# Eight of twelve modulation blocks formed by GpSimd in the weight ring instead of by TensorE

## The reference, cut to what matters

```python
mod = jax.nn.silu(c) @ w_ada[l] + b_ada[l]            # c: (1, 1024), w_ada: (1024, 6144)
shift1, scale1, gate1, shift2, scale2, gate2 = jnp.split(mod, N_MOD, axis=-1)
h = modulate(rms_norm(x, norm1_g[l]), shift1, scale1)
proj = h @ w_in[l]                                     # 5120 columns: q, k, v of two attentions, two gates
...                                                    # stick-breaking and block attention
x = x + gate1[:, None, :] * (merged @ w_out[l])
h2 = modulate(rms_norm(x, norm2_g[l]), shift2, scale2)
y = moe_ffn(h2, ...)                                   # 64 experts, 8 per token, and a shared one
x = x + gate2[:, None, :] * y
```

## Time and profile before

| | before |
|---|---|
| median of three runs | 1546.33 us (1545.08 to 1546.48) |
| the profiled execution | its span is recorded, 1541.1 us from the first to the last instruction; its own time beside that is not |
| PE busy | 1323.0 us, 86% of the span |
| DVE busy | 544.1 us, 35% |
| ACT busy | 406.4 us, 26% |
| POOL busy | 0.2 us, four small fills |
| loads and stores | 523.59 MB, mean 340 GB/s |

### The profile page before, as it was taken

The page is one execution under the profiler, slowest core; times in us unless marked ns, Lnnn a source line. Parts: engine busy times, 40 slices in busy tenths (PEclk is TensorE's granted clock), DMA queues, the critical chain, the costliest instruction groups (busy, mean ns, idle before and its releaser), DMA issues.

```text
span 1541.1 us, 26372 instructions
## 1 busy us (share of the span) xinstructions
PE 1323.0 (86%) x11246; PEld 939.5 (61%) x11246; DVE 544.1 (35%) x1189; ACT 406.4 (26%) x624; POOL 0.2 (0%) x4
## 2 busy tenths in 40 slices
PE   5999998999999999999799999999876557657646
PEld 2888896656667665556488999999633213213222
DVE  2546665443323232321375675763301001001001
ACT  3457753111121110101164346453301000000001
POOL 0000000000000000000000000000000000000000
PEclk8999999999999999999999999999989778778788
DMA  9984759799999999999953444746999999999995
GB/s 364 269 297 171 276 200 403 284 391 381 421 421 416 420 416 421 415 419 421 398 191 110 165 164 164 274 167 274 393 421 424 427 421 424 429 424 424 428 423 239
DMA packets 110254, 523.59 MB, mean 340 GB/s; under 512 B 10025, under 2 KB 14537, under 8 KB 71113
## 3 DMA queue, kind: packets, MB, share of 16 engines
q1 hardware_dynamic: 106880, 519.16, 84.4%
q10 hardware_dynamic: 3272, 2.96, 0.6%
HBM read 520.85 MB, written 1.24 MB: 339 GB/s over the span
## 4 chain that ended last, share of the span: by engine, by line
PE 61%; DMA 22%; SPq 10%; DVE 3%; ACT 2%; issue 1%; ACTq 0%; DVEq 0%
PE psum L2000 17%; DMA ring<-in_w_exp_up_dram 11%; PE psum L2455 10%; PE psum L2523 5%; DMA ring<-in_w_up_e_dram 5%; SPq L685 5%; SPq L689 4%; PE psum L2391 3%; PE psum L2380 3%; DMA arena<-in_w_exp_down_dram 2%; PE psum L2941 2%; DMA ring<-in_w_down_e_dram 2%; PE psum L2008 1%; PE psum L2252 1%; DMA ring<-in_w_exp_down_dram 1%; PE psum L2014 1%
## 5 line engine op out<-in xcount | busy, mean ns | idle before, releaser
L2000 PE MATMUL psum<-arena_r,ring_r 128*128 128x256 f32 x2176 | 272.5, 281 | 3.6 <-DVE arena_r L1164 3.1
L2000 PEld LDWEIGHTS psum<-arena_r,ring_r 128*128 128x128 f32 x2176 | 261.3, 188 | 8.8 <-issue 5.0
L2455 PE MATMUL psum<-ring,arena 128*32 128x256 f32 (+1 forms) x2304 | 183.9, 390 | 11.5 <-DMA ring<-in_w_up_e_dram 10.8
L1157 DVE TENSOR_TENSOR ring_r<-ring,ring_r 128x1024 fp32r<-128x1024 f32 x140 | 163.0, 1220 | 71.0 <-ACT ring_r L779 70.3
L2455 PEld LDWEIGHTS psum<-ring,arena 128*32 128x32 f32 (+1 forms) x2304 | 111.2, 123 | 76.4 <-issue 20.3
L2941 PE MATMUL psum<-ring,arena 128*32 128x256 f32 x1408 | 105.4, 454 | 54.3 <-DMA ring<-in_w_exp_gate_dram 27.6
L779 ACT ACTIVATE ring_r<-ring 128x1024 fp32r<-128x1024 f32 x140 | 137.4, 1050 | 27.9 <-DMA ring<-in_w_in_dram 12.7
L2958 PE MATMUL psum<-ring,arena 128*32 128x512 f32 x384 | 67.5, 866 | 56.6 <-DMA ring<-in_w_exp_down_dram 56.6
L2941 PEld LDWEIGHTS psum<-ring,arena 128*32 128x32 f32 x1408 | 48.4, 126 | 103.6 <-DMA ring<-in_w_exp_gate_dram 35.0
L2523 PE MATMUL psum<-ring,arena 128*32 128x512 f32 (+1 forms) x544 | 90.9, 617 | 3.1 <-DMA ring<-in_w_down_e_dram 2.2
L1935 DVE TENSOR_TENSOR arena<-arena,psum 128x256 f32<-128x256 f32 x16 | 6.7, 421 | 235.6 <-ACT arena L1116 235.6
(11 more groups left out here) (418 smaller groups left out, 1520.5 us busy)
## 6 DMA issues: line engine op xcount, KB each, us to landing
ring<-in_w_gate_e_dram SPq DMA_DIRECT2D x64, 1024.0 KB, 15.2
ring<-in_w_up_e_dram SPq DMA_DIRECT2D x64, 1024.0 KB, 14.3
ring<-in_w_down_e_dram SPq DMA_DIRECT2D x60, 1024.0 KB, 14.7
ring<-in_w_exp_gate_dram SPq DMA_DIRECT2D x29, 2048.0 KB, 32.0
ring<-in_w_exp_down_dram SPq DMA_DIRECT2D x48, 1024.0 KB, 30.1
ring<-in_w_in_dram SPq DMA_DIRECT2D x19, 2048.0 KB, 9.4
ring<-in_w_exp_up_dram SPq DMA_DIRECT2D x15, 2048.0 KB, 30.1
arena<-in_w_exp_up_dram SPq DMA_DIRECT2D x15, 2048.0 KB, 36.5
```

The lines of the kernel that those rows point to most:

```text
L1157: V.tensor_tensor(lo, whole, hi.bitcast(F32), ALU.subtract).then_inc(w_low, 1)
L2000: ins = product(lambda a_, b_, k, first, last: mm(ps[:, t * T:(t + 1) * T], a_[:, k, c], b_[:, k, :], start=first, stop=last), w, x, None ...
L2455: ins = mm(psum[c, 5, 256 * g:256 * g + 256], xg1[:, k, P * j + width * b:P * j + width * (b + 1)], weight(g, e, k), start=(k == 0), stop= ...
```

## The change

- For blocks 4 to 11, GpSimd multiplies each of the block's eight 128x512 pieces in its ring slot by silu(c) (eight `tensor_scalar`, in place), and adds the pieces as a tree: 128x2048, 128x1024 and 128x512. The last add writes a row buffer of 512. The semaphore `block_summed` counts the blocks.
- PE no longer makes the wide products of these blocks and ACT no longer copies them. PE's four one-column products stay; they now add 128 partial sums (a column of ones in the place of `sel_col`) and wait for `block_summed`. They come after in3 (block 4), after in5 (5) and after in6_0 to in9_0 (6 to 9); those of 10 and 11 stay where they were, and go straight into bank 7.
- Each block's load moves ahead: 4 behind w_in chunk 1, 5 behind 3, 6 to 10 behind 5 to 9; block 11 stays behind w_out. PE gives the slot's count back with the chunk before it, and whoever fills a slot that held such a block (SP, or ACT's copy) also waits for that block's sum.
- GpSimd waits before block j until the columns of block j-2 are done (for 10 and 11: until the last pair's scores `ss3` are), so that its row buffer is free.
- silu(c) overwrites c in the vector table; `mod[:, 40:48]` is read from bank 7, and PE waits for that read before `count1`.

```diff
-ADA_BEHIND = {2: (4,), 4: (5,), 6: (6,), 7: (7,), 8: (8,), 9: (9,)}
-ADA_PAIR = 6
+ADA_BEHIND = {1: (4,), 3: (5,), 5: (6,), 6: (7,), 7: (8,), 8: (9,), 9: (10,)}
+SUMMED_AFTER = {3: 4, 5: 5, 6: 6, 7: 7, 8: 8, 9: 9}
...
+        def block_left(eng, m):
+            if m - RING in SUMMED_SLOT:
+                eng.wait_ge(block_summed, SUMMED_SLOT[m - RING])
...
                     sp.wait_ge(used_a, SLOT_A[n] - RING + 1)
+                    block_left(sp, SLOT_A[n])
...
-                for n in ADA_BEHIND.get(c, ()):
-                    ada_copy(n)
...
-            copy_out("ada10", late_rows[0])
-            copy_out("ada11", late_rows[1])
...
+        @block.gpsimd
+        def _(pool):
+            G = nc.gpsimd
+            def block_sum(j):
+                n = SUMMED[j]
+                w = ring[:, SLOT_A[n] % RING, :].rearrange("p (k c) -> p k c", k=KT)
+                acc = summed[j]
+                if j < 10:
+                    pool.wait_ge(mod_full, j - 1)
+                else:
+                    full(pool, f"ss{PAIRS - 1}")
+                arrived(pool, ("a", n))
+                for k in range(KT):
+                    ins = G.tensor_scalar(w[:, k, :], w[:, k, :], csil[:, k:k + 1], None, ALU.mult)
+                ins.then_inc(part_ready, 1)
+                pool.wait_ge(part_ready, 3 * (j - ADA_FIRST) + 1)
+                G.tensor_tensor(w[:, 0:4, :], w[:, 0:4, :], w[:, 4:8, :], ALU.add).then_inc(part_ready, 1)
+                pool.wait_ge(part_ready, 3 * (j - ADA_FIRST) + 2)
+                G.tensor_tensor(w[:, 0:2, :], w[:, 0:2, :], w[:, 2:4, :], ALU.add).then_inc(part_ready, 1)
+                pool.wait_ge(part_ready, 3 * (j - ADA_FIRST) + 3)
+                G.tensor_tensor(acc, w[:, 0, :], w[:, 1, :], ALU.add).then_inc(block_summed, 1)
+            pool.wait_ge(csil_ready, 1)
+            for j in range(ADA_FIRST, ADA):
+                block_sum(j)
...
+            def columns(n):
+                place = psum[:, 7, 4 * ADA_ORDER[n]:4 * ADA_ORDER[n] + 4]
+                if n < ADA_FIRST:
+                    evacuated(pe, f"ada{n}")
+                else:
+                    pe.wait_ge(block_summed, n - ADA_FIRST + 1)
+                rows, col = (ada_rows[n % 2], sel_col) if n < ADA_FIRST else (summed[n], ones[:, 0:1])
...
-                held = (used_a, 2)
+                held = (used_a, 2 + len(ADA_BEHIND.get(c, ())))
...
-                for i, n in enumerate(ADA_BEHIND.get(c, ())):
-                    modulation(n, IN_A[c] + 1 + i, held)
-                    held = None
+                if c in SUMMED_AFTER:
+                    if c == 3:
+                        pe.wait_ge(mod_ready, 2)
+                    columns(SUMMED_AFTER[c])
...
-                columns(ADA_PAIR - 1 + p).then_inc(mod_full, 1)
+                columns(SUMMED_AFTER[6 + p])
...
-                modulation(ADA_PAIR + p, IN_A[6 + p] + 1, (used_a, 2))
...
-            modulation(ADA - 2, n0 + 14)
-            modulation(ADA - 1, n0 + 15, gives=(used_a, 1))
...
+            pe.wait_ge(mod_ready, 3)
             ps = start("count1")
```

More of the change, by code:

```diff
@@ L175 @@
 SLOT_A, NA = slots_of(CHUNKS_A, 0)
+SUMMED = {_j: CHUNKS_A.index(("w_ada", 512 * _j, 512, 8)) for _j in range(ADA_FIRST, ADA)}
+SUMMED_SLOT = {SLOT_A[_n]: _j - ADA_FIRST + 1 for _j, _n in SUMMED.items()}
 SLOT_B, NAB = slots_of(CHUNKS_B, NA)
@@ L292, in build @@
         pair_rows = [buf(12, 512, 512), buf(12, 512, 1024)]
-        late_rows = [buf(9, 512, 0), buf(9, 512, 512)]
+        late_rows = [buf(3, 512, 0), buf(3, 512, 512)]
+        summed = {_j: (ada_rows if _j < 6 else pair_rows if _j < 10 else late_rows)[_j % 2] for _j in range(ADA_FIRST, ADA)}
         onehot = buf(6, T, 768)
@@ L2076, in idle_products, with modulation @@
                     mm(ps[:, 0:T], ones, cst[:, 0:T], start=True, stop=True)
-            def columns(n, place=None, rows=None, gives=None):
-                evacuated(pe, f"ada{n}")
-                place = psum[:, 7, 4 * ADA_ORDER[n]:4 * ADA_ORDER[n] + 4] if place is None else place
-                rows = (pair_rows if n >= ADA_PAIR else ada_rows)[n % 2] if rows is None else rows
-                for b in range(4):
-                    ins = mm(place[:, b:b + 1], rows[:, b * P:(b + 1) * P], sel_col, start=True, stop=True)
-                    if gives is not None and b == 0:
-                        ins.then_inc(*gives)
-                return ins
-            def modulation(n, place, gives=None):
+            def columns(n):
[5 more added lines that the diff above has]
+                rows, col = (ada_rows[n % 2], sel_col) if n < ADA_FIRST else (summed[n], ones[:, 0:1])
+                for b in range(4):
+                    ins = mm(place[:, b:b + 1], rows[:, b * P:(b + 1) * P], col, start=True, stop=True)
+                ins.then_inc(mod_full, 1)
+            def modulation(n, place):
                 w = chunk_a(place, 512)
@@ L2097, in modulation @@
                                  start=(k == 0), stop=(k == 1))
-                        if gives is not None and k == 0 and q == 0:
-                            ins.then_inc(*gives)
                 done(ins, f"ada{n}")
-                if ADA_PAIR <= n < ADA - 2:
-                    return
-                if ADA_FIRST < n < ADA - 2:
-                    columns(n - 1, gives=(used_a, 1)).then_inc(mod_full, 1)
-                elif n != ADA - 2:
-                    full(pe, f"ada{n}")
-                    used(used_a, 1)
-                if n == ADA_FIRST:
-                    pe.wait_ge(mod_ready, 2)
+                full(pe, f"ada{n}")
+                used(used_a, 1)
             def norm_sums(name, sqb, ready):
@@ L2259, in _ @@
             ws = chunk("a", n0 + 10, whole=False)
-            branch("brs_0", ws, 0, 0, range(3), SPLIT_AT[("a", n0 + 10)], gives=(used_a, 1))
-            columns(ADA - 3).then_inc(mod_full, 1)
+            branch("brs_0", ws, 0, 0, range(3), SPLIT_AT[("a", n0 + 10)], gives=(used_a, 3))
             attend(PAIRS - 1)
```

51 lines of the change are left out of this document (27 added, 24 removed).

## The result

| | before | after |
|---|---|---|
| median | 1546.40 us (1545.08 to 1547.11, 4 runs) | 1578.62 us (1576.05 to 1581.24, 4 runs) |
| ratio to before | | 1.0214, 95% interval 1.0197 to 1.0230 |
| profiled span | 1541.1 us | 1575.7 us |
| end of the first stage: logit1 starts on PE at | 250.54 | 285.73 |

What follows compares the result with a forecast made beforehand. The prediction took PE to set the time, with VectorE almost without room in the pairs. 17.3 lost against 13.3 gained made 4.0 slower, 1545.1 of span, plus 5.2 around it: 1550 us, range 1532 to 1572.

Steps and rivals of the forecast that it cites:

- Removed from PE, 13.3: First stage: wide products 11.2, waits 0.5 and 0.8, one-column products 0.8 leave PE's chain; 13.3 us gained.
- Added on GpSimd, 9.1 us a block: Eight scalings at ACT's 0.60 and adds at VectorE's rate: 4.8 + 4.3 = 9.1 us a block, eleven instructions.
- The upper end that the forecast kept, 57: Most a GpSimd block could take: all 7680 elements at the slowest row, RECIPROCAL's 0.95 per 128; 57 us.
- GpSimd beside VectorE, 17.3: VectorE waits for GpSimd's instructions: 12.8 over four pairs and 4.5 ahead of them, 17.3 us lost.
- an even 0.62 an instruction: Mean wait w of each affected VectorE instruction on GpSimd, three quarters of the upper end 0.83.
- Rival 3, the sums are late, chance 0.08: PE's one-column products wait for block sums; at 28 us a block 24 late, 11 slower, 1557; chance 0.08.
- Its threshold, 20 us a block: Blocks 7, 8 and 9 have 59 us for their three sums, so up to 20 each is in time.
- Its price, three for each us from block 5's place on: Above 20 us a block, every microsecond of a block costs PE three.
- Loads: SP's queue: loads reusing a slot wait for its block's sum, delaying those behind; each comes in time, no cost.
- mod_ready ahead of count1: PE's new wait ahead of count1 is for an instruction that ends before PE gets there: nothing.
- the shift that carries to the end: Expert loads wait for the item table PE's chain makes, so a shift of the first stage carries to the end.
- 5.2 around the span: Time outside the profiled span: median 1546.33 against span 1541.1, if a median run; 5.2 us added at the end.

Runs made afterwards that it cites:

- beside the kernel before: Kernel before, with GpSimd doing the eleven instructions seven times on a buffer nobody waits for; ratio 1.0118, logit1 at 267.64, 17.1 later than before.
- two parts: Changed kernel with three adds without scalings (logit1 251.92), and with scalings and last add (240.87), against last add alone (238.00): adds 13.9, scalings 2.9.
- the quiet late run: Changed kernel with the two larger adds replaced by five more scalings; ratio 1.0152, logit1 at 272.84, 32.0 later than with eight scalings.
- scalings and last add: Changed kernel with the two larger adds of each block left out; ratio 0.9919, logit1 at 240.87.
- the one between: Changed kernel with the two larger adds replaced by three extra scalings; ratio 1.0048, logit1 at 261.47.

## Why the prediction was wrong, step by step

- *Removed from PE, 13.3:* right; 12.5 measured.
- *Added on GpSimd, 9.1 us a block:* **this step failed.** It priced a scaling at ACT's 0.60 for the same shape and the adds at VectorE's rate, 4.3. Measured: 1.91 a scaling, 15.2 a block, and 9.2 for the adds; 25 with what lies between. Undisturbed a scaling took 1.56 and a block 21.3; that VectorE would lengthen GpSimd's instructions in turn was foreseen, but not priced into the block. The upper end that the forecast kept, 57, held. Taking the nearest row of another engine was the error; nothing in the trace of before had GpSimd computing. The Trainium skill's figures (GPSIMD Engine Reference, Elementwise — side-by-side cycle accounting) were nearer: its 4497 ns for a 2048-element add agrees with 4.63, while its 769 ns for a 512-element pass does not agree with a scaling's 1.91, or 1.56 undisturbed.
- *GpSimd beside VectorE, 17.3:* the size was right (17.1 beside the kernel before; 16.8 as two parts), by errors that cancelled. GpSimd's instructions are not alike: the scalings cost 2.9, the adds 13.9. And the loss is not an even 0.62 an instruction; it is a few waits as long as a GpSimd instruction, one of which breaks a pair and slows the clock behind it. The exclusion that the Trainium skill states (SBUF — State Buffer, Who interferes with whom) is what these rows show for two-input GpSimd instructions; beside scalings, which read SBUF too, the low parts kept 2.42 for two, and the two scalings took 4.25 instead of 3.1, so there it was GpSimd that waited.
- *Rival 3, the sums are late, chance 0.08:* this came true on top of the forecast. The two add up: 16.8 lost less 12.5 gained is 4.3 (the forecast had 4.0), and the quiet late run gives 32.0, less about 2 for its extra scalings, for lateness: 34 of the 35.2. That the sum comes out so near is in part luck: each term is read from one execution, and the 3.3 that block 11's adds cost ahead of logit1 is in none of these runs. The prediction treated them as alternatives though they hang on the same price. Its threshold, 20 us a block, fits: one block every 17.5 us (scalings and last add) was in time, every 22.2 (the one between) was not. Its price, three for each us from block 5's place on, was too low: at 25.5 it gives 16, and the quiet late run lost 30. GpSimd runs without a gap from block 4's load, and a late sum also holds the loads behind it on SP's queue and ScalarE's copies.
- *Loads:* "a late sum delays all that follow" was foreseen with the condition that it would come in time; in6's load was the first to show it. The list of such loads left out block 9's, which takes block 7's slot: six loads waited, 71.4 in all. *mod_ready ahead of count1, and the shift that carries to the end:* right, 1290.6 against 1290.0 behind logit1.
- *5.2 around the span:* not borne out. The profiled execution after took 1577.5 with a span of 1575.7, so 1.8 around it; the profiled execution before was probably some 3 quicker than its median, and so the spans differ by 34.6 where the medians differ by 32.2.

## What to carry to other kernels

Before work moves to an idle engine, ask how long one unit takes there and how often a unit is needed: a unit of 25 us against a pair of 19 makes the idle engine the bound, and everything that waits for its buffers follows its pace. An engine that shares its way into SBUF with a busy one costs by the length of its single instructions and by their sum, so it is cheap only where the busy engine has room; here that was two blocks of eight. Cases that hang on one uncertain price belong in one sum, not side by side as rivals.

## What the runs showed of the hardware

- On GpSimd a two-input product with a broadcast operand is quicker than a scaling by a per-partition scalar: 1.04 against 1.56 for 128x512 where neither met a VectorE instruction (1.26 against 1.89 in the mean), 7.0 against 12.4 for a block.
- A VectorE instruction with two SBUF inputs waited until the GpSimd add or product in flight was through (5.4 of the 7.02 us product at 123.27). The other way round, adds of 128x512, 1.26 at their shortest, averaged 1.9 beside a busy VectorE, and of the change's 27 scalings beside a low part 13 took 2.7 or more instead of 1.56, while low parts beside scalings alone averaged 1.29 instead of 1.22.
- A gap of 4.9 on PE cost 2.6 more in the next 5.87 us product, which began at a granted clock of 0.50; idle products that raised the clock in two windows of three won nothing.
